# Four low halves on GpSimd and a new order of every engine's work in the mixers and at two norms

## What is computed

```python
def first_block(x, ...):
    h = rms_norm(x, norm_mix_pre)
    proj = h @ w_in                       # iq, ik, iw, k, v, q, xr, gr, g_a, g_b
    y_rnn = rg_lru(causal_depthwise_conv(xr, conv_w, conv_b), ...) * gelu(gr)
    y_att = dsa_sparse_attention(q, k, v, iq, ik, iw)      # 16 heads
    merged = sigmoid(g_a) * (y_rnn @ w_rnn_out) + sigmoid(g_b) * (y_att @ w_att_out)
    x = x + rms_norm(merged @ w_o, norm_mix_post)          # norm "f0": this sum
    h = rms_norm(x, norm_ffn_pre)                          #            and this norm
    x = x + rms_norm((silu(h @ w_ffn_gate) * (h @ w_ffn_up)) @ w_ffn_down, norm_ffn_post)
    return x

def second_block(x, ...):
    for l in range(2):
        x = x + 0.5 * swiglu(rmsnorm(x, ffn1_norm[l]), ...)     # norm "f1" for l = 0
        mix = (even_mixer if l % 2 == 0 else odd_mixer)(rmsnorm(x, norm[l]))
        x = x + mix
        x = x + 0.5 * swiglu(rmsnorm(x, ffn2_norm[l]), ...)
    return x
```

## Time and profile before

| | us |
| --- | --- |
| median of 3 executions | 1405.13 (1404.22 to 1405.39) |
| the profiled execution: its own time | 1404.55 |
| the profiled execution: span, first to last instruction | 1402.7 |
| TensorE busy | 1380.0 (98% of the span) |
| VectorE busy | 967.4 (69%) |
| ScalarE busy | 811.2 (58%) |
| GpSimd busy | 53.6 (4%) |
| mean granted clock of TensorE | 0.998 of full speed |

### The profile page before, as it was taken

The page is one execution under the profiler, slowest core; times in us unless marked ns, Lnnn a source line. Parts: engine busy times, 40 slices in busy tenths (PEclk is TensorE's granted clock), DMA queues, the critical chain, the costliest instruction groups (busy, mean ns, idle before and its releaser), DMA issues.

```text
span 1402.7 us, 19388 instructions
## 1 busy us (share of the span) xinstructions
PE 1380.0 (98%) x7290; PEld 1177.4 (84%) x7290; DVE 967.4 (69%) x1472; ACT 811.2 (58%) x1264; POOL 53.6 (4%) x62
## 2 busy tenths in 40 slices
PE   8999999999999999999999999999999999999999
PEld 7898788788887888888788888888888877888887
DVE  6999846667755767657976777556775594667753
ACT  6679954565644555545766555445554576565541
POOL 2021000000000000000000000000000070000000
PEclk9999999999999999999999999999999999999999
DMA  9544445466665666566346665666655540366551
GB/s 306 178 126 135 152 153 186 140 213 193 184 193 166 192 182 194 186 189 198 112 158 200 191 186 190 189 187 183 192 189 187 161 140 27 121 211 193 185 192 60
DMA packets 127212, 242.63 MB, mean 173 GB/s; under 512 B 7568, under 2 KB 13328, under 8 KB 127120
## 3 DMA queue, kind: packets, MB, share of 16 engines
q1 hardware_dynamic: 126208, 239.15, 55.1%
q0 software_dynamic: 624, 2.10, 0.5%
q10 hardware_dynamic: 288, 0.14, 0.0%
HBM read 240.31 MB, written 1.05 MB: 172 GB/s over the span
## 4 chain that ended last, share of the span: by engine, by line
PE 93%; DVE 4%; ACT 2%; issue 1%; DMA 0%; SPq 0%; ACTq 0%; DVEq 0%
PE PX L347 24%; PE PX L378 16%; PE PX L380 16%; PE PX L379 16%; PE PX L344 12%; PE PX L424 3%; PE PX L669 2%; PE PX L558 1%; DVE WL L329 1%; PE PX L372 1%; PE PX L374 1%; PE PX L373 1%; PE PX L562 0%; ACT WH L323 0%; DMA X<-in_x_dram 0%
## 5 line engine op out<-in xcount | busy, mean ns | idle before, releaser
L329 DVE TENSOR_TENSOR WL<-RAW,WH 128x1024 fp32r<-128x1024 f32 (+2 forms) x454 | 555.1, 1228 | 352.1 <-ACT WH L323 350.2
L323 ACT ACTIVATE WH<-RAW 128x1024 fp32r<-128x1024 f32 (+2 forms) x454 | 477.1, 1053 | 503.1 <-PE PX L380 267.1
L347 PE MATMUL PX<-AT,WH 128*128 128x512 f32 x1440 | 361.3, 393 | 0.0
L347 PEld LDWEIGHTS PX<-AT,WH 128*128 128x128 f32 x1440 | 259.2, 189 | 46.6
L378 PE MATMUL PX<-WH,AT 128*128 128x512 f32 (+4 forms) x528 | 210.3, 398 | 6.0 <-DVE AT L1329 6.0
L344 PEld LDWEIGHTS PX<-AT,WL 128*128 128x128 f32 x1440 | 196.4, 190 | 14.1
L380 PE MATMUL PX<-WH,AT 128*128 128x512 f32 (+4 forms) x528 | 201.8, 382 | 0.0
L379 PE MATMUL PX<-WL,AT 128*128 128x512 f32 (+4 forms) x528 | 201.2, 381 | 0.0
L344 PE MATMUL PX<-AT,WL 128*128 128x256 f32 x1440 | 200.8, 282 | 0.0
L378 PE MATMUL PX<-WH,FTh 128*128 128x512 f32 x440 | 171.5, 390 | 0.0
L379 PE MATMUL PX<-WL,FTh 128*128 128x512 f32 x440 | 171.2, 389 | 0.0
(11 more groups left out here) (333 smaller groups left out, 1328.5 us busy)
## 6 DMA issues: line engine op xcount, KB each, us to landing
RAW<-in_ffn_w_gu_dram SPq DMA_DIRECT2D x132, 512.0 KB, 3.7
RAW<-in_ffn_w_gu_2b_dram SPq DMA_DIRECT2D x88, 512.0 KB, 3.7
RAW<-in_w_in_dram SPq DMA_DIRECT2D x44, 512.0 KB, 3.8
RAW<-in_ffn_w_down_dram SPq DMA_DIRECT2D x44, 512.0 KB, 3.3
RAW<-in_ffn_w_down_2b_dram SPq DMA_DIRECT2D x44, 512.0 KB, 3.3
RAW<-in_w_ffn_down_dram SPq DMA_DIRECT2D x22, 512.0 KB, 3.6
RAW<-in_ev_w_in_dram SPq DMA_DIRECT2D x20, 512.0 KB, 3.7
RAW<-in_w_rnn_out_dram SPq DMA_DIRECT2D x8, 512.0 KB, 3.7
```

The lines of the kernel that those rows point to most:

```text
L323: e.activation(WH[i % NHL][:, 0:m], RAW[i % NRAW][:, 0:m], ACT.Copy).then_inc(*up("hi", i))
L329: e.tensor_tensor(WL[i % NHL][:, 0:m], RAW[i % NRAW][:, 0:m], WH[i % NHL][:, 0:m].bitcast(F32), ALU.subtract).then_inc(*up("lo", i))
L347: ins = e.matmul(PB[bank].rearrange("p (h s) -> p h s", h=2), w[:, f], AT0B[:, :, k, :], start=k == p.k_lo, stop=False, skip_group_check=True)
```

## The change

The change has two parts.

1. The low halves of chunks 76 and 77 (norm f0) and of 142 and 143 (norm f1) are computed by GpSimd instead of VectorE. It is the same subtraction. They count on a semaphore of their own, `lo_p`, since two engines now produce low halves; whoever waits for a low half (TensorE's passes, and `load` of the chunk six further on) picks the semaphore by `LOW(i)`. On GpSimd they stand behind `pool_post` of their norm.
2. The lists of all engines in the first, the even and the odd mixer and at norms f0 and f1 are written in another order. The steps are the same, except that ScalarE loads its tables 26 times instead of 23: once more in the first mixer and twice more in the even one.

In the new file lines behind the helpers are 12 further down: `L1281` of before is `L1293` of after, `L1283` `L1295`, `L1286` `L1298`, `L1329` `L1341`; the subtraction `L329` is now `L334`.

```diff
+        POOL_LOW = [F[f][0][0].first + x for f in (0, 1) for x in (2, 3)]
+        def LOW(i):
+            return "lo_p" if i in POOL_LOW else "lo"
+        def low(e, i):
+            m = stream[i][2] * stream[i][4]
+            e.wait_ge(*on("hi", i))
+            e.tensor_tensor(WL[i % NHL][:, 0:m], RAW[i % NRAW][:, 0:m], WH[i % NHL][:, 0:m].bitcast(F32),
+                            ALU.subtract).then_inc(*up(LOW(i), i))
         def lo(e, i):
-            if i < len(stream):
...
+            if i < len(stream) and i not in POOL_LOW:
+                low(e, i)
+        def pool_lo(e, f, x):
+            low(e, F[f][0][0].first + x)
...
# pool_program
             pool_post(e, "f0")
+            pool_lo(e, 0, 2)
+            pool_lo(e, 0, 3)
             pool_post(e, "f1")
+            pool_lo(e, 1, 2)
+            pool_lo(e, 1, 3)
...
# pe_first_mixer
-            dense(e, IKW, 0, 5)
+            dense(e, IKW, 0, 2)
             pe_in_spread(e)
-            dense(e, IKW, 5, 6)
+            dense(e, IKW, 2, 6)
...
+            dense(e, GR0, 0, 16)
+            pe_gates(e, 1)
+            pe_gates(e, 2)
             pe_scores(e, AT_A, 2)
...
+            dense(e, GR1, 0, 16)
             pe_turn_p(e, AT_A, 0)
...
-            dense(e, WO[1], 0, 8)
+            dense(e, WO[1], 0, 7)
             pe_turn_block(e, 'f0', 0, 0)
+            dense(e, WO[1], 7, 8)
             pe_turn_block(e, 'f0', 0, 1)
-            dense(e, F[0][0][0], 0, 2)
+            dense(e, F[0][0][0], 0, 4)
             pe_turn_block(e, 'f0', 1, 0)
-            dense(e, F[0][0][0], 2, 3)
             pe_turn_block(e, 'f0', 1, 1)
-            dense(e, F[0][0][0], 3, 4)
             dense(e, F[0][0][1], 0, 2)
...
# act_first_mixer
             hi(e, 6)
+            act_in_diag(e)
             act_iq(e, 0)
             act_iq(e, 1)
-            hi(e, 7)
-            act_in_diag(e)
-            hi(e, 8)
...
# dve_post_norm
+            lo(e, 142)
+            lo(e, 143)
             dve_post_root(e, 'f1', 0)
-            lo(e, 142)
             dve_post(e, 'f1', 0, 0)
             dve_post(e, 'f1', 0, 1)
-            lo(e, 143)
-            lo(e, 144)
             dve_block_lo(e, 'f1', 0, 0)
+            dve_post_root(e, 'f1', 1)
             dve_block_lo(e, 'f1', 0, 1)
-            dve_post_root(e, 'f1', 1)
...
# dve_even_mixer
-            dve_diff(e, AT_B, 0)
-            dve_diff(e, AT_B, 1)
-            dve_max(e, AT_B, 3)
...
# dve_odd_mixer
             dve_gqa_sums(e)
+            dve_gqa_root(e)
             lo(e, 377)
-            dve_gqa_root(e)
...
             dve_mla_sums(e, 1)
-            lo(e, 384)
             dve_mla_root(e)
```

More of the change, by code:

```diff
@@ L2251, in pe_first_mixer @@
             pe_scores(e, AT_A, 6)
-            pe_values(e, AT_A, 2)
-            dense(e, GR0, 12, 15)
+            pe_scores(e, AT_A, 7)
             pe_turn_p(e, AT_A, 3)
-            dense(e, GR0, 15, 16)
-            dense(e, GR1, 0, 2)
-            pe_gates(e, 2)
+            dense(e, GA0, 7, 8)
+            pe_values(e, AT_A, 3)
+            dense(e, GA1, 0, 7)
             pe_turn_p(e, AT_A, 4)
-            pe_values(e, AT_A, 3)
-            dense(e, GR1, 2, 5)
+            dense(e, GA1, 7, 8)
@@ L2581, in act_first_mixer @@
             hi(e, 24)
+            hi(e, 25)
+            hi(e, 26)
+            act_xr(e, 0, 0)
+            act_xr(e, 0, 1)
+            act_conv(e, 0, 0)
+            act_conv(e, 0, 1)
+            hi(e, 27)
             act_keys1(e, 0)
@@ L2606, in act_first_mixer @@
+            act_conv(e, 3, 1)
+            act_root(e, 1)
+            hi(e, 36)
+            hi(e, 37)
+            hi(e, 38)
+            act_gr(e, 1, 0)
+            act_exp(e, AT_A, 0)
+            act_gates(e, 2)
+            act_p(e, AT_A, 0)
+            act_y(e, 0)
+            act_decay(e, 2)
+            act_gr(e, 1, 1)
+            hi(e, 39)
+            hi(e, 40)
             act_exp(e, AT_A, 1)
             act_exp(e, AT_A, 2)
-            act_gates(e, 1)
             act_p(e, AT_A, 1)
-            act_decay(e, 1)
+            hi(e, 41)
@@ L2645, in act_first_mixer @@
-            act_root(e, 3)
+            act_decay(e, 3)
+            act_p(e, AT_A, 3)
             act_ga(e, 0, 0)
             act_ga(e, 0, 1)
-            hi(e, 41)
+            act_root(e, 3)
+            hi(e, 42)
+            hi(e, 43)
+            hi(e, 44)
+            hi(e, 45)
+            act_exp(e, AT_A, 4)
+            hi(e, 46)
+            act_p(e, AT_A, 4)
+            act_ga(e, 1, 0)
+            act_ga(e, 1, 1)
+            hi(e, 47)
+            act_exp(e, AT_A, 5)
             act_exp(e, AT_A, 6)
+            act_p(e, AT_A, 5)
@@ L2697, in act_first_mixer @@
             act_o_hi(e, 3)
+            act_y(e, 3)
+            hi(e, 55)
             hi(e, 56)
@@ L3045, in dve_first_mixer @@
             dve_conv(e, 2, 1)
+            lo(e, 30)
+            lo(e, 31)
+            lo(e, 32)
+            lo(e, 33)
+            lo(e, 34)
+            dve_conv(e, 1, 1)
+            dve_max(e, AT_A, 0)
+            lo(e, 35)
+            dve_max(e, AT_A, 1)
+            dve_max(e, AT_A, 2)
             dve_gx(e, 1)
@@ new lines, in dve_first_mixer @@
+            dve_conv(e, 3, 1)
+            dve_input(e, 0)
+            lo(e, 36)
+            dve_scan(e, 0)
+            lo(e, 37)
+            dve_y(e, 0)
+            lo(e, 38)
+            dve_gx(e, 2)
+            dve_input(e, 1)
+            dve_decay(e, 2)
+            dve_ylo(e, 0)
+            lo(e, 39)
+            lo(e, 40)
+            dve_scan(e, 1)
+            lo(e, 41)
+            dve_max(e, AT_A, 4)
+            dve_gx(e, 3)
+            dve_max(e, AT_A, 5)
+            dve_max(e, AT_A, 6)
@@ L3067, in dve_first_mixer @@
+            dve_decay(e, 3)
+            dve_out(e, AT_A, 0)
+            dve_max(e, AT_A, 7)
+            dve_input(e, 2)
+            dve_scan(e, 2)
+            lo(e, 42)
+            lo(e, 43)
+            lo(e, 44)
+            lo(e, 45)
+            lo(e, 46)
+            dve_input(e, 3)
+            lo(e, 47)
+            dve_scan(e, 3)
+            lo(e, 48)
+            dve_max(e, AT_A, 8)
+            lo(e, 49)
             dve_y(e, 1)
-            dve_max(e, AT_A, 5)
-            lo(e, 37)
+            dve_max(e, AT_A, 9)
```

690 lines of the change are left out of this document (310 added, 380 removed).

## The result

| | before | after |
| --- | --- | --- |
| median, us | 1405.08 (1404.22 to 1407.16, 9 executions) | 1410.70 (1408.13 to 1412.24, 9 executions) |
| profiled execution, span | 1402.7 | 1407.9 |
| mean granted clock | 0.998 | 0.996 |

A forecast was written before the change was run, and what follows sets the result against it. TensorE was taken as the bound (93% of the chain), with time won only where it stands or runs at half clock. Terms -3.5 - 0.7 - 2.4 + 0.9 + 0.8 + 0.3 = -4.6 us gave 1400.5 us, range 1396.8 to 1406.5.

The forecast's parts named there:

- Norm f0: At norm f0: VectorE starts first, TensorE starts earlier and no half clock is expected; -3.5 us.
- Norm f1: At norm f1: a tie, taken with VectorE first, but root 1 waits for GpSimd; -0.7 us, +0.3 with GpSimd first.
- The start: At 19.6 us: `pe_in_spread`, four passes earlier, waits for a DMA-dependent chain; +0.9 us (0 to 1.2).
- First mixer: In the first mixer: new waits and one more table load against old small waits that go; net +0.8 us (-2 to +4).
- `gates(1)`: In the first mixer, behind GR0: waits for the last high half, its low half and one convolution; +1.0 us.
- `turn_p(0)`: In the first mixer, behind GR1: waits for a copy, the table load and the exponentials; +1.4 us.
- the next two waits: In the first mixer, the two new waits after `turn_p(0)`; together +0.8 us.
- ScalarE as the bound, my slower rival: First mixer: exponentials lose cover and ScalarE stalls TensorE, +5.8 us, 1409.0 us with other waits; chance 0.14.
- Even mixer: In the even mixer: two more table loads while TensorE doesn't wait for ScalarE, nothing to win; +0.3 us (0 to 1.5).
- Odd mixer: In the odd mixer: low half of 384 moves behind the long root, transposes start earlier, clock need not fall; -2.4 us.
- the part behind it: Later part of the odd mixer, two output groups ahead of the fourth unit's scores; gives or takes 0.6 us.
- the GpSimd-first case: Norms f0 and f1: GpSimd wins the race or is slow, terms -1.2 and +0.3, 1403.8 us; chance 0.13.

The follow-up runs named there:

- first_only: Kernel before with only the first mixer's lists of after, start included, all low halves on VectorE; 1411.38 us, ratio 1.0034.
- f0_only: Kernel before with only norm f0 changed (lists, low halves of chunks 76 and 77 on GpSimd); 1402.09 us against 1404.64, ratio 0.9981.
- first_conv_early: first_only with VectorE's last convolution ahead of gates(1) moved from behind the low half of chunk 34 to ahead of that of chunk 30; ratio 1.0019.
- odd_only: Kernel before with only the odd mixer's lists of after, all low halves on VectorE; ratio 1.0012.
- odd_max_early: Kernel before with VectorE's long root in the odd mixer moved behind the maxima of units 4 and 5; 1401.71 us against 1404.96, ratio 0.9980.
- lows_only: Kernel before with only the low halves of chunks 76, 77, 142 and 143 moved to GpSimd, every list as before; 1408.92 us, ratio 1.0032.

## Why the prediction was wrong, point by point

- **Norm f0, -3.5: right.** The segment measures -3.3 to -3.6. VectorE came first, GpSimd took 2.38 and 2.40 us for a low half that had not to wait (rows at f1; 2.5 assumed), `L1298` waited and `L1295` did not, no half clock. That VectorE won by "a hair" (0.08 us between the rows) was luck. And 1.7 us of the gain is the half clock of the earlier trace rows, which not every execution of the old lists has: in first_only the clock did not fall at f0, and the segment is -1.4 with nothing changed there. By the ratio f0_only gains 2.7 us.
- **Norm f1, -0.7: wrong side of a tie.** GpSimd won, and the term was the +0.3 that I had worked out for that case; +0.27 measured. With the tie decided the other way, -0.6. Neither counts the falls of the clock at f1 (see the base, below).
- **The start, +0.9: right in the profile** (+0.82), but the wait's size is the DMA's. With the old lists it is anything from too short to be listed to 2.0 us, with the new ones 0.3 to 2.1.
- **First mixer, +0.8 (-2 to +4): the failed step.** I had priced `gates(1)` at +1.0, by the chain high half, low half, convolution at 1.5 us. The convolution took 3.42 us, as GpSimd's squares ran beside it: the same lock that I had weighed at the norms, and did not look for here, though the earlier trace rows show it and the squares were in GpSimd's list. So TensorE waited 2.94 us at `gates(1)`, and the fall of the clock behind it cost 1.7 more, which I had not added to any new wait. `turn_p(0)`, priced at +1.4, waited 1.44 and was followed by another fall (1.7). The stretch of the convolution (1.9) and the two falls are 5.3 us; the next two waits, priced at 0.8, took 0.4. That makes 4.9, against an error of this term of 4.6 us (+5.4 for +0.8, beyond the 4 us that I had named as a sign of being wrong). ScalarE as the bound, my slower rival, did not happen: it was busy 60.6 us of the 75 from 85 to 160 us, against 69.9 before. It was the one late at `turn_p(0)`, but by the place of the exponentials and their table load in its list; shortly ahead of them (121.63) it had stood idle for 1.8 us. The misplaced convolution, for which my theory after the result took the whole loss, is worth some 2 us of the +4.8 of first_only, by first_conv_early.
- **Even mixer, +0.3 (0 to 1.5): too small,** +1.4; 0.8 of it is the wait for norm f2's addition, the rest is spread over waits under 0.3 us and I have not traced it.
- **Odd mixer, -2.4: wrong sign,** +0.7. The step "the low half of 384 moves behind the root, so the root ends 1.3 us earlier" failed. The root ended at 1162.86, with the stage 4.2 us late as a whole, so 0.1 us later than before: the head sum ahead of it (`L1859`) now waited 0.50 us for GpSimd's squares, these for ScalarE's last query copy, which came at 1155.02 instead of 1149.77, 1.0 us more than the stage was late. The 1.2 us of new idle time ahead of the turn were priced right and cost nothing, as I had said. The 1.7 us of the clock did come back behind the fourth unit, but the part behind it, which I had put at 0.6 us either way, lost 2.6 us: the turn came 4.3 us late and net 4's third group 5.2, although before has its half clock (1.7) in between. 1.7 of them are the five small waits, the rest I have not traced. My sentence that a clock fall needs over 2 us of standing was a rule drawn from three cases: it fell behind 1.16 us in after, and did not behind 1.17 us in odd_only. That the long root held unit 4 only by its place in the list I had not seen either; it is worth 2.8 us.
- **The base.** I set the sum against one profile, and there read "after 2.74 us at f1 the clock did not fall" as a property of f1. The earlier trace rows stopped 0.6 us behind that wait; the longer window confirms it for that execution only. The clock fell there in seven of the nine profiles with the lists of before and that wait of 2.74 us (not in before itself and in odd_max_early); these are the seven segments of +1.6 to +2.9. It did not in any of the four with the new lists. In lows_only it fell, too, behind longer waits.
- **The range.** Its upper end does not follow from its own words: the GpSimd-first case with its spread ends at 1403.8 + 1.5 = 1405.3, not 1406.5. The result lies beyond both.

## What to carry to other kernels

When steps are moved between lists, ask for every one of them what GpSimd is doing at its new time: a short two-operand VectorE step can take three times as long beside it (0.48 and 1.50 us for a step of the convolution), and all that is queued behind comes late. Count each new TensorE wait of over a microsecond with a possible fall of the clock (1.7 to 2.8 us here), and each old one removed likewise; a profile of one execution shows only one draw of that. Where an engine waits, look first for a step ahead in its releaser's list that the release doesn't need: that single move gave 2.8 of the 6.9 us of the best gain here, while the new lists of each of the three mixers gave a loss.

## What was not expected of the hardware

The granted clock behind the same stall, with the same instructions around it, was 1.00 over six microseconds in one execution and 0.53 in another, behind the same 2.74 us (norm f1). It fell to 0.60 over four microseconds behind standing only 1.16 us, between short transposes and products of 64 columns, and stayed at 1.00 behind the same 1.17 us in odd_only. A one-column VectorE step (0.15 us alone) took 1.68 us beside a GpSimd operation on other tiles. And a VectorE row can start 0.02 us ahead of GpSimd's and still have lost the ports, as the 2.94 us at f1 show, while 0.08 us were enough at f0: at such margins the row's start does not tell who came first.
